# Second block's mixer: the gate strips and the linear attention set between the strips of the input projection

## The reference

```python
for l in range(2):
    h = h + 0.5 * swiglu(rmsnorm(h, g[l, 0]), ...)
    h = h + mixer(rmsnorm(h, g[l, 1]), ...)
    h = h + 0.5 * swiglu(rmsnorm(h, g[l, 2]), ...)

def mixer(z, w_in, ...):
    (q_a, k_a, v_a, r_a, lr_f, lr_b, q_b, k_b, v_b, g_a, g_b) = split(z @ w_in)
    a = gla_branch(q_a, k_a, v_a, r_a, lr_f, lr_b, ...)      # linear attention, 4 heads, both directions
    b = attention_branch(q_b, k_b, v_b, q_norm, k_norm, ...) # softmax attention, 8 heads, 2 key heads
    y = (sigmoid(g_a + b_merge[0]) * (a @ w_pa)
         + sigmoid(g_b + b_merge[1]) * (b @ w_pb))
    return y @ w_out

def gla_causal_chunked(q, k, v, log_a):   # chunks of 64 tokens
    bcum = cumsum(log_a)                                     # in each chunk
    q_dec, k_inv, k_end = q * exp(bcum), k * exp(-bcum), k * exp(btot - bcum)
    o_intra = where(mask, q_dec @ k_inv.T, 0) @ v
    S = decay[chunk] * S + k_end.T @ v                       # from chunk to chunk
    return o_intra + q_dec @ S_prev
# then o * rsqrt(mean(o * o)) * gain * silu(r_a); q_b and k_b get rmsnorm and a rotation
```

## Time and profile before

| | us |
|---|---|
| median of 3 runs (4550.11 to 4564.77) | 4553.85 |
| the profiled execution | 4556.2 |
| its span | 4554.4 |
| PE busy | 3954.7 (87%) |
| DVE busy | 2106.3 (46%) |
| ACT busy | 1440.3 (32%) |
| mean granted clock of PE | 0.897 of full |

### The profile page before, as it was taken

The page is one execution under the profiler, slowest core; times in us unless marked ns, Lnnn a source line. Parts: engine busy times, 40 slices in busy tenths (PEclk is TensorE's granted clock), DMA queues, the critical chain, the costliest instruction groups (busy, mean ns, idle before and its releaser), DMA issues.

```text
span 4554.4 us, 66722 instructions
## 1 busy us (share of the span) xinstructions
PE 3954.7 (87%) x25210; PEld 3491.5 (77%) x25210; DVE 2106.3 (46%) x2554; ACT 1440.3 (32%) x1891; POOL 398.9 (9%) x410
## 2 busy tenths in 40 slices
PE   7856999695699969999769989998999957999997
PEld 6335877552478759998648989998999946898997
DVE  4446773444577444424345444424433345445433
ACT  2133551212355223412233324313332233323331
POOL 0203110220211020000002000000000001100000
PEclk9757999885799989999869989998999967999998
DMA  3001222210122222222101222222222200122222
GB/s 124 32 1 46 97 92 94 86 54 0 37 83 96 90 68 92 87 92 86 33 1 22 90 70 87 92 91 80 92 88 90 83 1 1 61 83 74 92 87 84
DMA packets 106329, 314.02 MB, mean 69 GB/s; under 512 B 29984, under 2 KB 29984, under 8 KB 105984
## 3 DMA queue, kind: packets, MB, share of 16 engines
q1 hardware_dynamic: 104800, 303.22, 20.3%
q0 software_dynamic: 1440, 9.61, 0.6%
HBM read 310.62 MB, written 2.10 MB: 69 GB/s over the span
## 4 chain that ended last, share of the span: by engine, by line
PE 81%; DVE 11%; ACT 4%; issue 2%; SPq 1%; POOL 1%; DMA 1%; DVEq 0%; ACTq 0%; POOLq 0%
PE acc L1343 68%; DVE x_lo L735 2%; PE misc L1691 1%; DVE sumsq L729 1%; PE misc L1343 1%; PE acc L1452 1%; PE misc L1418 1%; PE acc L1662 1%; PE misc L1427 1%; SPq L328 1%; PE acc L1673 1%; PE acc L1678 1%; PE acc L1594 1%; PE misc L1469 1%; DVE maxima L813 1%
## 5 line engine op out<-in xcount | busy, mean ns | idle before, releaser
L1343 PE MATMUL acc<-x_hi,w_hi 128*128 128x264 f32 (+1 forms) x5092 | 1295.1, 317 | 209.8 <-DVE x_lo L735 180.1
L1343 PE MATMUL acc<-x_lo,w_hi 128*128 128x264 f32 (+1 forms) x5092 | 1282.1, 315 | 0.0
L1343 PE MATMUL acc<-x_hi,w_lo 128*128 128x264 f32 (+1 forms) x5092 | 1278.2, 314 | 0.0
L364 ACT CAST w_hi<-stage 128x1024 fp32r<-128x1024 f32 x570 | 598.2, 1050 | 1916.1 <-PE acc L1343 1847.3
L1343 PEld LDWEIGHTS acc<-x_hi,w_hi 128*128 128x128 f32 x5092 | 846.3, 192 | 305.9 <-issue 172.4
L707 DVE TENSOR_TENSOR w_lo<-stage,w_hi 128x1024 fp32r<-128x1024 f32 x570 | 765.3, 1343 | 592.2 <-ACT w_hi L364 582.4
L1343 PEld LDWEIGHTS acc<-x_hi,w_lo 128*128 128x128 f32 x5092 | 846.1, 193 | 51.4
L1343 PEld LDWEIGHTS acc<-x_lo,w_hi 128*128 128x128 f32 x5092 | 846.5, 192 | 50.7 <-issue 1.8
L1343 PE MATMUL acc<-ff_hi,w_hi 128*128 128x264 f32 (+1 forms) x1760 | 429.3, 309 | 32.7 <-POOL ff_lo L1243 16.5
L1343 PE MATMUL acc<-ff_hi,w_lo 128*128 128x264 f32 (+1 forms) x1760 | 428.1, 308 | 0.0
L1343 PE MATMUL acc<-ff_lo,w_hi 128*128 128x264 f32 (+1 forms) x1760 | 427.9, 308 | 0.0
(11 more groups left out here) (265 smaller groups left out, 3836.2 us busy)
## 6 DMA issues: line engine op xcount, KB each, us to landing
stage<-weights SPq DMA_DIRECT2D x570, 512.0 KB, 3.2
rotary_decay<-tables POOLq DMA_DIRECT2D x2, 2048.0 KB, 7.7
consts<-consts POOLq DMA_DIRECT2D x4, 704.0 KB, 4.7
x<-x_in SPq DMA_DIRECT2D x1, 2048.0 KB, 8.4
max_rows<-max_columns SPq DMA_DIRECT2D x128, 0.5 KB, 2.0
out<-x SPq DMA_DIRECT2D x1, 2048.0 KB, 7.0
rotary_masks<-tables POOLq DMA_DIRECT2D x2, 784.0 KB, 4.8
params<-params POOLq DMA_DIRECT2D x2, 279.0 KB, 3.2
```

The costliest lines, as they stand in the source:

```text
L364: nc.scalar.copy(whi[p][:, :], stage[p][:, :]).then_inc(hi_ready, 1)
L1343: ins = mm(ps[:, b, 0:tn], ww, act_[:, kt, t0:t0 + tn], start=start and n == 0 and q == 0, stop=stop and n == last and q == 2)
```

## The change

- The 16 gate strips leave `merge` and join the input projection, whose strips become 35 (the spare one goes); `merge` has 8 strips. A buffer `gates` (GT) of 16 tiles keeps the gates until then.
- The strips of the projection come in another order: decay logits, q and k of the linear attention, its values, then k, q, v of the softmax attention, `r_a`, gates.
- `gated`, the norms and the preparation of queries and keys become pieces in `mixer2`, set by hand between the strips, on PE, DVE, ACT and POOL.
- The 35 strips all use `acc0` (`one_slot`): strip k+1 waits until strip k is brought out. `acc1` serves the pieces.
- Within a piece the linear attention goes head by head, where it went by pairs. The key is rotated once (it was turned and rotated per key head, four products of 528 tokens), and copied per head by ACT.
- `mix_hi` and `mix_lo` are now `x_hi` and `x_lo` themselves.
- ACT's tables: the joint set for logarithm and exponential is chosen ahead of its uses, the tables for the feed-forward once ahead of each loop.

```diff
-IN2 = 20
-MERGE2 = 3 * KT
+IN2 = 35
+MERGE2 = KT
...
-PAIRS2 = (0, 4, 1, 2, 3)
+PAIRS2 = (4, 0, 1, 2, 3)
...
+        mh, ml = xh, xl
         E1, E2 = sq[:, 0, :], sq[:, 1, :]
-        QC, RI2 = (rY, ss), (rY, ss)
+        RI2 = (rY, ss)
+        QSQ, QR, QSIN, QC = (GT[:, 9, :], GT[:, 10, :]), (GT[:, 11, :], GT[:, 12, :]), GT[:, 13, :], (GT[:, 14, :], GT[:, 15, :])
...
-            def choose_table(function):
-
-                chain(nc.scalar.activation(first_use[:, :], eps_c, function))
+            def logs_and_exps():
+
+                nc.scalar.preload_act_table_set("natural_log_exp_and_others")
...
                 norm_in(TALL, gcol, False)
-                with loop(act, FT, [(stg[0], 16), (stg[1], 16), (free, 2), (ev, 2), (prod, 1), (steps, 1)]) as m:
-                    choose_table(ACT.Silu)
+                nc.scalar.preload_act_table(ACT.Silu)
+                with loop(act, FT, [(stg[0], 16), (stg[1], 16), (free, 2), (ev, 2), (prod, 1)]) as m:
                     split_hi()
...
-                with loop(act, 4, [(stg[0], 48), (stg[1], 48), (free, 6), (ev, 6), (prod, 2)]) as i:
-                    for a in range(2):
-                        for g, buf in enumerate((G0, G1)):
-                            split_hi()
-                            wait_evacuated()
-                            nc.scalar.activation(buf[:, :], buf[:, :], ACT.Tanh, scale=0.5,
-                                                 bias=gain(G_BM + 8 * g + a, 2 * i)).then_inc(gate_act, 1)
-                        split_hi()
-                        wait_evacuated()
-                        act.wait_ge(prod_ready, prod.up())
-                        nc.scalar.activation(tile_of(yh, 2 * i + a, TALL), T0[:, :], ACT.Copy, scale=0.5).then_inc(fh_ready, 1)
+                for c in range(KT):
+                    for g in range(2):
+                        nc.scalar.activation(GT[:, 2 * c + g, :], GT[:, 2 * c + g, :], ACT.Tanh, scale=0.5,
+                                             bias=gain(G_BM + 8 * g, c)).then_inc(gate_act, 1)
+                    split_hi()
+                    wait_evacuated()
+                    act.wait_ge(prod_ready, prod.up())
+                    nc.scalar.activation(yh[:, c, :], T0[:, :], ACT.Copy, scale=0.5).then_inc(fh_ready, 1)
...
+            def one_slot():
+
+                dve.wait_ge(strip_done, data.up())
+                return acc[0]
+
+            def strip_out(dst, n=P):
+
+                link(nc.vector.tensor_tensor(like(dst, TALL), view(one_slot(), TALL, n), like(rB[0:n, :], TALL), ALU.mult),
+                     evacuated, ev)
...
+                chain(nc.vector.memset(LR[32:64, :], 1.0))
+                strip_out(LR[0:32, :], 32)
+                split_lo()
+                strip_out(QKO[:, 0, :])
+                split_lo()
+                strip_out(QKO[:, 2, :])
+                split_lo()
+                log_gate(0)
+                strip_out(QKO[:, 1, :])
+                split_lo()
+                for t in range(1, 5):
+                    log_gate(t)
+                strip_out(QKO[:, 3, :])
+                split_lo()
+                decayed(0)
...
+                strip_out(QKV[:, 0, :])
+                chunk_decays(0, 0)
+                chunk_decays(0, 1)
+                split_lo()
+                states(0, 0)
+                strip_out(QKV[:, 1, :])
+                split_lo()
+                states(0, 1)
+                scale(0)
+                strip_out(QKV[:, 2, :])
+                masked(0, 0)
+                masked(0, 1)
+                split_lo()
+                rope(0)
...
+                def one_slot():
+                    pe.wait_ge(evacuated, ev.up() + 1)
+                    return acc[0]
+
+                def strip_of(per_tile=None):
+                    multiply([([(k, xh, xl, k) for k in range(KT)], one_slot(), T)], per_tile=per_tile)
...
+                strip_of(lambda: pe.wait_ge(xl_ready, xlr.up()))
+                stats(T)
+                strip_of()
+                pe.wait_ge(param_in, prm.up(16))
+                gate_logits()
+                for _ in range(3):
+                    strip_of()
+                for dm in range(4):
+                    cumulated(dm)
+                    strip_of()
+                for t in range(5):
+                    keys_turned(t)
+                strip_of()
+                for t in range(5):
+                    values_turned(t)
+                strip_of()
+                chunk_states(0, 0)
+                chunk_states(0, 1)
+                strip_of()
+                mean_square(0)
+                strip_of()
+                rotated(0)
+                intra(0, 0)
+                intra(0, 1)
+                strip_of()
+                mean_square(1)
+                intra_out(0, 0)
+                intra(0, 2)
+                intra_out(0, 1)
+                strip_of()
+                rotated(1)
+                intra_out(0, 2)
+                inter_out(0)
+                intra(1, 0)
+                intra(1, 1)
...
+                head_square(3)
+                for _ in range(6):
+                    strip_of()
+                pe.wait_ge(q_rope, at(5, 5))
+                pe.wait_ge(go_evac, at(4, 4))
                 for t, (c0, n) in enumerate(TILES2):
-                    dst = acc[0][0:n, 0, (t - 1) * P:t * P] if t else acc[0][0:n, 1, 0:P]
+                    dst = M[0:n, 0, (t - 1) * P:t * P] if t else M[0:n, 1, 0:P]
                     ins = nc.tensor.transpose(dst, QKV[:, 5, c0:c0 + n], ident)
                 ins.then_inc(vt2_full, 1)
-
-                def mean_square(i):
-                    pe.wait_ge(q_sq, at(5, i + 1))
-                    if i >= 2:
-                        pe.wait_ge(q_ln, at(5, i - 1))
-                    rows(M[:, 2 * (i % 2):2 * (i % 2) + 2, :], blk, sq[:, i % 2, :]).then_inc(q_ms, 1)
-
-                def rotated(i):
-                    j = PAIRS2[i]
-                    pe.wait_ge(q_n, at(5, i + 1))
-                    if j >= 2:
-                        pe.wait_ge(q_sin, at(4, j - 1))
-                    rows(acc[j % 2], con[:, K2_PQ:K2_PQ + P], QKV[:, j, :]).then_inc(q_rot, 1)
-
-                mean_square(0)
-                mean_square(1)
-                pe.wait_ge(vl2_ready, at(1, 1))
-                rotated(0)
-                pe.wait_ge(q_n, at(5, 2))
-                pe.wait_ge(q_ln, at(5, 2))
-                for kv in range(2):
-                    if kv:
-                        pe.wait_ge(k_cos, at(2, kv))
-                    rows(M[:, 0:2, :], con[:, K2_E0 + kv * P:K2_E0 + (kv + 1) * P], QKV[:, 4, :])
-                    rows(M[:, 2:4, :], con[:, K2_S0 + kv * P:K2_S0 + (kv + 1) * P], QKV[:, 4, :]).then_inc(k_rot, 1)
-                pe.wait_ge(k_cos, at(2, 2))
-                mean_square(2)
-                mean_square(3)
-                rotated(2)
-                mean_square(4)
-                rotated(3)
-                rotated(4)
-                pe.wait_ge(q_sin, at(4, 4))
-                pe.wait_ge(q_ln, at(5, 5))
+                for _ in range(3):
+                    strip_of()
+                all_evacuated()
...
-                with loop(pe, 4, [(hi, 6), (lo, 6), (ev, 6)]):
-                    for a in range(2):
-                        project(TALL)
-                        project(TALL)
-                        s = next_slot()
-                        multiply([([(k, mh, ml, k) for k in range(4)], s, TALL),
-                                  ([(k, mh, ml, k) for k in range(4, 8)], M[:, 2:4, :], TALL)])
+                pe.wait_ge(gl_ready, at(4, 4))
+                for c in range(KT):
+                    multiply([([(k, mh, ml, k) for k in range(4)], next_slot(), TALL),
+                              ([(k, mh, ml, k) for k in range(4, 8)], M[:, 2 * (c % 2):2 * (c % 2) + 2, :], TALL)])
```

More of the change, by code:

```diff
@@ new lines, in mixer2 @@
+                split_hi()
+                g_inverse(2)
+                split_hi()
+                g_inverse(3)
+                split_hi()
+                for h in range(4):
+                    g_tanh(h)
+                logs_and_exps()
+                split_hi()
+                act.wait_ge(q_rope, at(5, 1))
+                k_hi(0)
+                k_hi(1)
+                split_hi()
+                q_hi(0)
+                q_hi(1)
+                split_hi()
+                q_hi(2)
@@ L603, in probs, with attention2 @@
+                split_hi()
+                split_hi()
+                split_hi()
+                for h in range(4):
+                    g_hi(h)
+                ev.up(IN2)
+            def attention2(T=TALL):
+                act.wait_ge(gl_ready, at(4, 4))
                 def probs(n):
@@ new lines, in states @@
+                def states(mt, d):
+                    dm = 2 * d + mt
+                    dve.wait_ge(kv_read, at(4, dm_order(mt, d) + 1))
+                    for c in (range(1, 8) if d == 0 else range(6, -1, -1)):
```

(11 more changed lines are left out.)

813 lines of the change are left out of this document (489 added, 324 removed).

## The result

The changed kernel takes 4417.0 us (median of 4 runs, 4416.4 to 4420.4) against 4555.2 us (4550.1 to 4564.8): ratio 0.9695, interval 0.968 to 0.9711. It is faster by 138 us where 180 were forecast. 4417 lies inside the whole range (4345 to 4440) and outside the forecast's own (4357 to 4405), so the direction and the mechanism held, about a quarter of the gain is missing, and it is the wider range that takes the result in. The profiled execution has a span of 4414.5 us (before 4554.4).

What follows compares the result with a forecast made beforehand. PE bounds the kernel (busy 87%), so time leaves where it idles or runs slower. From 4556.2, 150.5 for mixers and 28.9 for tables gave 4376.8, stated as 4375 us; own range 4357 to 4405, whole 4345 to 4440.

Steps and rivals of the forecast that it cites:

- the sign: Among the signs of being right: `merge`, left with 8 strips, takes about 48 us.
- 150.5 were forecast: Both mixers: stretches without strips of 156.3 and 154.4 us gained, 80.1 us paid per mixer, so 150.5 us less.
- The payment of 62 for the pieces: PE's products between strips cost 62 us a mixer, between 55 and 92.
- the 70 that the prediction itself had set as a sign of being wrong: Strip stage: products per head that take over 70 us a mixer would show the forecast wrong.
- The clock rival: Strip stage: short gaps lower the mean clock to 0.85, costing 48 us a mixer, 4472 us; chance 0.08.
- Strip 2 was charged at 2.3 us: Strip 2 waits for strip 1's evacuation, which needs the norm: logarithm, exponential, evacuation and hand-offs, 2.3 us a mixer.
- A gap: Nine strips with no piece before them each wait 0.9 us for the previous evacuation, 8.1 us a mixer.
- The end of the attention: From first `maxima` to `merge` nothing changes, 120.2 us; first `maxima` starts about 5.4 us after strip 35.
- The allowance of 3.0 a mixer for misfit: Strip stage: 3.0 us a mixer for strips delayed by DVE's other instructions standing between evacuations.
- The tables: Fewer activation-table loads at norms, feed-forward loops, head norms and retention: 28.9 us less; about 60 with the skill's drain.
- late evacuations: Rival: in-order DVE slips, 20 of 35 strips lose 1.5 us, 30 a mixer, 4435 us; chance 0.15.
- PE at 1.2 GHz: Rival, slower than before: waits for the only accumulator hold the strip stage at half clock, 4925 us; chance 0.04.

Runs made afterwards that it cites:

- mixed: The changed kernel with the 8 score products of heads 1 and 3 set between the 16 state products of heads 0 and 2: 4410.1 us, ratio 0.9672.
- The kernel again: The changed kernel run again as it is, in the last series: 4419.0 us, ratio 0.9695.
- the three with 9 steps: Scores 9 instead of 8 steps ahead: in the changed kernel 4409.7 us, with three other edits 4375.9, with those and state products of heads 1, 3 halved 4371.4.

## Why the prediction was right, and where its sizes were off

**What held.** The mechanism, the sign and most of the sum. Strips ran while ACT and DVE worked on the linear attention, the strip stage is one stretch of PE work (281 of 292 us), and `merge` fell to 49.9 us (about 48 was the sign). The mixers gained 61.4 and 53.4 us (from the norm's sums to the out-projection 529.8 to 468.4 and 528.8 to 475.4), 114.8 where 150.5 were forecast. Outside them 25 us came in place of 28.9.

**The payment of 62 for the pieces was mis-sized.** It took a head's state products at half of the pair's price in the earlier trace rows, and counted it as nearly nothing that neighbours no longer alternate between the halves of the array. Four groups of 3.71 us stand where two of 3.79 did: 7.3 us a mixer, 14.5 of the 35.7 missing. The order turned in the kernel before shows it (112 ns from record to record for 56, everything else equal), and mixing wins 1.17 us of it back a time. This term is the step that failed: the sum named the lost neighbour, had no row for it, and took 62, a value in which it costs nothing. With the falls, the bare gaps and strip 2 taken off, the strips with pieces are 73 us over the bare price in either mixer, where the sum has 62. That is over the 70 that the prediction itself had set as a sign of being wrong; some 4 us of it belong to no cause that a run singled out.

**The clock rival was dismissed on the wrong ground.** It asked whether gaps of 0.9 us bring the clock down, and they don't: strips 28 to 35, with a gap ahead of each, ran at 6.91 to 7.03 us throughout. What brings it down here is a busy piece of state products, with no gap in it. Whether it is that they read half of the partitions, or that they are small as well (64x64, each with its own load of 64x128), no run separates; the gate logits read the same half and bring no fall. That costs three steps of 1.5 us a mixer in the first trace and five in the second, 9 us in all in the first. The two other orders (mixed, halved) and the kernel without the products have fewer falls, and only these groups are changed there.

**Strip 2 was charged at 2.3 us and costs 4.7** (period 8.42 against 3.74): 2.9 of waiting and 1.75 because the strip behind it runs partly at half clock. 4.8 us in both mixers. It is the wait that the change put in, since before it two accumulators alternated there.

**A gap costs 1.05 us, not 0.9** (6.92 against 5.87): 9 x 0.15 = 1.4 us a mixer.

**The end of the attention** was taken as unchanged at 120.2 us. In the first mixer it is near (121.85 with the 5.4 of waiting in it, 3.8 less than forecast), in the second 15.7 us at half clock cost 6 of the 6.7 more. The kernel before had such falls too, in another mixer, so a single profiled execution can't carry this term closer than 6 us a mixer. The kernel again and the three with 9 steps show both halves: it comes and goes with the execution, and it stays away without the wait.

Together the strip stage is 32.8 us over its 275.3 (16.7 and 16.1). Of these, 14.5 + 9 + 4.8 + 2.7 = 31.0 are named above. The allowance of 3.0 a mixer for misfit was not needed for what it was meant for, as no strip waited for a mask or a state; it went into the 4 us of the pieces that stay unexplained. From strip 35 to `merge` it is 3.8 under in one mixer and 3.0 over in the other, and the rest of each mixer, `merge` above all, 1.9 over the 52.7 that the sum implied: 35.8 us against 35.7 missing.

**The tables** were right within what runs can tell: 28.9 forecast, 24.5 measured (17 to 29). The changed kernel's own trace shows 17.2 in the first block where the tables alone show 22.6 with the same code there; executions differ by as much (1657.55 to 1662.99). By the drain that the Trainium skill states ("ScalarE: Activation LUTs", What ACT_TABLE_LOAD costs) the same edits should have given about 60 us, an estimate. No run here shows it: in the earlier trace rows the activation starts when the load of 1.28 us ends, and the measured gain is near the 28.9 that the loads alone would give.

**Of the rivals,** late evacuations and PE at 1.2 GHz did not occur. The Trainium skill ("TensorE: Matmul & The Clock Gate", A second HAM failure mode: psum-queue depth-cycling) tells of a kernel that cycles through PSUM banks and whose clock swings with the short idle times between groups of products. Here, with one accumulator and a wait at each bare strip, it did not: 0.98 over the stage, and no fall in strips 28 to 35.

## What to carry to other kernels

In this kernel the small products that read 64 partitions were cheap only beside a neighbour that reads the other 64. Before such work is reordered, look which half each neighbour reads, and interleave two groups rather than run them one behind the other. Where freed idle time is filled, read the clock at each place and not only the mean of the stage: a gain at one place may return as a longer fall of the clock at the next such group, as it seems to have done with strip 2. And read such falls from several executions: the same code had three steps of them a mixer in one and five in the next.

## What the runs showed of the hardware that was not expected

- The granted clock fell to 1.2 GHz while PE was busy without a gap, 3 us into a group of state products on one half of the partitions (112 ns from record to record at full clock, 213 at half), or right behind such a group of 3.7 us. With the group in halves a strip apart, most of the falls are gone. Behind 4.6 us of gate logits on the same half, with 512 columns each, there is none.
- A wait of 1.42 us in the attention was followed by 15.7 us of full work at half clock; one of 0.91 us in another mixer of the same execution was not, yet one of 0.92 us at the same place in the next execution was. Gaps of 0.8 us ahead of nine strips left the clock alone.
- A strip that starts from standstill takes 6.13 us for 5.88. By the timeline 0.10 of it is at the first pair of products (0.35 us to the next pair for 0.245), and 0.16 at the last, whose end has no next pair beside it.
- The same kernel's profiled spans differ by 9.9 us (4414.5 and 4424.4), and the falls alone account for 6.2 us in the strips and 6.5 in the first mixer's attention; a start of the second block that is 3.6 us earlier works against them.
